# Latent heads' output projection in three rounded terms, split beside the first projection

## Chip, cores and metric

The kernel runs on one core of one Trainium2 chip. The time is the device time of one execution in microseconds (us), given as the median of three runs. A profiled execution gives the trace; its own time stands beside it below. Engines are named as in the profile: PE is TensorE (PEld its weight loads), DVE VectorE, ACT ScalarE, POOL GpSimd, SP SyncE, which issues the weight loads.

## The reference

Two transformer layers (a dense feed-forward network in the first, eight experts in the second) are followed by a third block of another kind. All values are float32, 256 tokens of 1024 features. What the change touches is the same in both layers:

```python
o_na  = neighborhood_attention(...)          # 8 heads of 64: 256 x 512
o_mla = latent_attention(q_mla, k_mla, ...)  # 8 heads of 64: 256 x 512
merged = (sigmoid(g_na  + b_gate[i, :D_MODEL]) * (o_na  @ w_na_o[i])
        + sigmoid(g_mla + b_gate[i, D_MODEL:]) * (o_mla @ w_mla_o[i]))
x = _layer_norm(DEEPNORM_ALPHA * x + merged @ w_out[i], ln1_g[i], ln1_b[i])
```

## The kernel before

Activations lie feature-major: a tile is 128 features by 256 tokens, and `o_na` and `o_mla` are four such tiles each. Each engine runs a program written out by hand, and semaphores tie them together; nothing else sets the order. Weights come through a ring of five slots of 128 x 4096 floats that SP fills in the order of `layer_plan`; a slot's next load waits until the semaphore that marks its last use has come.

Most products are made in "three rounded terms": a weight w and an input x are each split into a rounded part (type fp32r, "short") and the remainder ("rest"), and PE adds short x short, short x rest and rest x short. Making the short part is a copy (ACT, DVE or POOL), making the rest is a subtraction (DVE or POOL), written in place over the weights in the ring (`ring_lo`, `weights_rest` in the profile). A few products are still plain float32 matmuls, which the profile records as two entries each; they go through the helper `product` (L905).

After the sixteen attention heads, worked off in pairs, each layer makes sixteen output-projection tiles on PE: eight of `o_na` with `w_na_o`, then eight of `o_mla` with `w_mla_o`, each of four plain float32 matmuls (`heads_tiles`). They go into two PSUM banks in turn (`dve_bank`): a tile may start when DVE has finished with the tile two before it (`dve_tile_done`). Two tiles of `o_na` are made before the last pair's value products (L998), the others after.

DVE copies the value products out of PSUM (`output`, L2221), the last pair's as the last step of `attention`. Then it multiplies each `o_na` tile by its gate (L2528), and for each `o_mla` tile multiplies by the gate (L2542), adds the two (L2543, after which the bank is free), rounds the sum (L2535) and makes its rest (L2539), the latter two one and two tiles late.

ACT meanwhile takes the sigmoid of both gate tensors (L1847), makes `alpha_ident` for the residual (L1848) and the short parts of the first two halves of `w_out` (L1855); POOL subtracts to get their rests (L803), waiting for `act_w_short`. On PE, `residual_rows` (L1042) and `merged_rows` (L1056) follow the sixteenth tile.

Of the kernel before, what the change touches and what calls it, by code (L numbers as in the profile page):

```python
# [32 lines left out]
ACT = mybir.ActivationFunctionType  # L33
AX_X = mybir.AxisListType.X

P = 128
SEQ = 256
QT = SEQ // P
D = 1024
DT = D // P  # L40
# [55 lines left out]
RING = SLOTS - 2  # L96
IN_UNITS = 6 + 4 + 8
# [143 lines left out]
def build(nc, t):  # L241
    with ExitStack() as ctx:
# [6 lines left out]
        def parts(name, of, shape, first=0):  # L249

            return nc.alloc_sbuf_tensor_at(name, shape, F32R, offset=base_of[of] + 4 * first)

        def sem(name):
            return ctx.enter_context(nc.semaphore(name))


        ring = sb("weight_ring", [P, SLOTS, SLOT])
# [7 lines left out]
        probs = sb("probs", [P, 2, QT, SEQ])  # L265
# [18 lines left out]
        def tiles(ap, n):  # L284
            return ap.rearrange("p (t s) -> p t s", t=n)

        def const(name):
            return consts[:, slice(*CONST_AT[name])]
# [4 lines left out]
        ring_lo = [parts(f"weights_rest{i}", "weight_ring", [P, SLOT], SLOT * i) for i in range(SLOTS)]  # L293
# [16 lines left out]

        in_x = [parts(name, "weight_ring", [P, DT, SEQ], SLOT * RING + 2048 * i) for i, name in enumerate(("layer_in_short", "layer_in_rest"))]
        lat_x = [parts("latents_short", "arena_o", [P, DT, SEQ]), parts("latents_rest", "probs", [P, DT, SEQ])]
        in_w = [parts(f"layer_weights_short{b}", "weight_ring", [P, 2048], SLOT * (RING + 1) + 2048 * b) for b in range(2)]

        ff_silu = arena_mla[:, 2048:3072].rearrange("p (b s) -> p b s", b=2)
# [121 lines left out]
        first_rows_here = sem("first_rows_here")  # L437
        y_stored, y_picked, y_summed = sem("y_stored"), sem("y_picked"), sem("y_summed")
        put_picked, put_turned, put_ready = sem("put_picked"), sem("put_turned"), sem("put_ready")
        last_y, last_scattered, turn_added = [sem(f"last_y{i}") for i in range(2)], sem("last_scattered"), sem("turn_added")  # L440
        y_weighed, place_moved = sem("y_weighed"), sem("place_moved")
        moe_x_short, moe_x_ready = sem("moe_x_short"), sem("moe_x_ready")
# [113 lines left out]
        ple_block_at = [loads_of(plan) - 3]  # L556
# [81 lines left out]
        def weights_landed(block):  # L638
            return weights_here[block % RING], 32 * (block // RING + 1)
# [235 lines left out]
        def _(pe):  # L875
            n = Counts()

            def weights(k, cols, landed=True):

                i = n.block  # L880
                n.block += 1
                if landed:
                    pe.wait_ge(weights_here[i % RING], 32 * (i // RING + 1))
                return ring[:, i % RING, 0:k * cols].rearrange("p (k n) -> p k n", k=k)
# [375 lines left out]
            for l in range(LAYERS):  # L1260
# [70 lines left out]
                def heads_tiles(o, j0, j1):  # L1331
                    for j in range(j0, j1):
                        product(dve_bank()[:, 0:SEQ], cols(heads_w[-1], j * P, (j + 1) * P), k_tiles(o, 4)).then_inc(dve_tile_ready, 1)
# [14 lines left out]
                assert layer_turn_ps[l][1] is dve_ps[(n.d + 1) % 2]  # L1348
                attention(layer_pairs * l, layer_pairs, beside_pair, layer_turn_ps[l])
                heads_tiles(o_na, 2, DT)  # L1350
                heads_w.append(weights(4, D))
                pe.wait_ge(out_copied, layer_pairs * (l + 1))
                heads_tiles(o_mla, 0, DT)
                residual_rows(l)
                merged_rows(l, lambda k: (merged_split, DT * l + k + 1))
                i = n.block
# [259 lines left out]
        def _(act):  # L1616
# [181 lines left out]
            for l in range(LAYERS):  # L1798
# [46 lines left out]
                act.wait_ge(act_tile_done, n.a)  # L1845
                for g in gates:
                    nc.scalar.activation(g[:, :, :], g[:, :, :], ACT.Sigmoid).then_inc(merge_gates_ready, 1)  # L1847
                nc.scalar.activation(alpha_ident, const("ident"), ACT.Copy, scale=ALPHA).then_inc(alpha_ready, 1)  # L1848
                units = layer_units(l)

# [229 lines left out]
        def _(dve):  # L2080
# [3 lines left out]
            def ready():  # L2084
                i = n.d
                n.d += 1
                dve.wait_ge(dve_tile_ready, i + 1)
                return dve_ps[i % 2]
# [65 lines left out]
            def rms_norm(out, src, gain):  # L2154

                for j in range(DT):
                    V.scalar_tensor_tensor(out[:, j, :], src[:, j, :], gain[:, j:j + 1], std[:, 1, :], ALU.mult, ALU.mult)\
                        .then_inc(rms_ready, 1)

            def attention(first, pairs, between=None, fill=None, ahead=None, lag=1):  # L2160
                def maxima(a):
                    j = jobs[a]
# [47 lines left out]
                            m = V.tensor_scalar(p, p, rinv[:, b, i:i + 1], None, ALU.mult)  # L2210
                    m.then_inc(probs_ready, 1)

                def output(p):
                    j = jobs[2 * p]
                    dve.wait_ge(pv_ready, p + 1)
                    src = out_ps[:, p % 2 * SEQ:(p % 2 + 1) * SEQ]
                    if j["add"]:
                        dve.wait_ge(out_copied, p)
                        V.tensor_tensor(j["out"], j["out"], src, ALU.add).then_inc(out_copied, 1)
                    else:  # L2220
                        V.tensor_copy(j["out"], src).then_inc(out_copied, 1)  # L2221

                for p in range(pairs + 1):
                    at = 2 * (first + p)
                    if lag == 2 and 2 <= p < pairs:
# [11 lines left out]
                            fill(p)  # L2237
                    if lag == 1 and p:
                        output(first + p - 1)
                for p in range(pairs - 2, pairs if lag == 2 else 0):  # L2240
                    output(first + p)

            a_tiles = [0]

# [214 lines left out]
            for l in range(LAYERS):  # L2459
# [64 lines left out]
                attention(layer_pairs * l, layer_pairs, fill=lambda p: in_rest(l, 11) if p == 0 else gate_rest(l, p + 1) if p < layer_pairs - 1 else None, lag=2)  # L2524
                act_tiles(QT + 2 * DT)
                dve.wait_ge(merge_gates_ready, 2 * l + 1)
                for j in range(DT):
                    V.tensor_tensor(merged[:, j, :], ready()[:, 0:SEQ], gates[0][:, j, :], ALU.mult).then_inc(dve_tile_done, 1)  # L2528
                dve.wait_ge(merge_gates_ready, 2 * l + 2)
                merged_at = n.d  # L2530

# [351 lines left out]
```

## Time and profile before

| | us |
|---|---|
| median of 3 runs | 2029.85 |
| lowest and highest | 2029.56, 2030.17 |
| profiled execution, its own time | 2030.13 |
| its span in the trace | 2028.3 |
| PE busy | 1990.2 (98% of the span) |
| DVE busy | 1535.9 (76%) |
| ACT busy | 1012.3 (50%) |
| POOL busy | 79.9 (4%) |

The profiled execution's time is its span and 1.8 us around it. Busy shares are means over many stages. The stretch that matters here is some 35 us long and comes twice, about 170 to 207 us and 614 to 651 us from the span's start.

### The profile page before, as it was taken

To read this page: it belongs to the slowest core of one execution; us is meant where nothing else is said; L and a number is where in the kernel's file an instruction comes from. 1 tells how busy PE (TensorE), PEld (TensorE's weight loads), DVE (VectorE), ACT (ScalarE), POOL (GpSimd) and SP (SyncE) were. 2 spreads that over 40 slices of the span, in tenths; PEclk is the share of its full clock that TensorE was granted. 3 is DMA by queue.
4 is the path that set the end of the run, shared out by engine and by line. 5 is a ranking of instruction groups with operands and counts; after the bars stand their busy time and mean duration, and the time that the engine had idled before them with its cause. 6 is when DMAs were issued, how large, how long until landed. Compare 5 with 4: busy or idle time off the path is not lost.

```text
span 2028.3 us, 28426 instructions
## 1 busy us (share of the span) xinstructions
PE 1990.2 (98%) x11368; PEld 1714.6 (85%) x11368; DVE 1535.9 (76%) x1541; ACT 1012.3 (50%) x1064; POOL 79.9 (4%) x57
## 2 busy tenths in 40 slices
PE   8999999999999989999999999999999998999999
PEld 8988799989988778888888888888888877869998
DVE  3674677776654698888888888888888976567766
ACT  0363110011452377777777777777777753472000
POOL 0111100000001200000000000000001000100000
PEclk9999999999999999999999999999999999999999
DMA  9643588744634689999999999999999984435550
GB/s 328 197 152 110 184 297 307 270 148 129 218 125 151 235 297 384 381 379 371 385 385 375 385 381 380 370 384 385 377 384 380 408 284 151 145 105 178 196 176 33
DMA packets 184221, 553.22 MB, mean 273 GB/s; under 512 B 9296, under 2 KB 112080, under 8 KB 140864
## 3 DMA queue, kind: packets, MB, share of 16 engines
q1 hardware_dynamic: 175296, 517.55, 69.7%
q10 hardware_dynamic: 6912, 25.02, 3.0%
q0 software_dynamic: 1920, 9.34, 1.2%
q8 instruction: 66, 1.08, 0.2%
q14 instruction: 27, 0.22, 0.0%
HBM read 528.02 MB, written 23.59 MB: 272 GB/s over the span
## 4 chain that ended last, share of the span: by engine, by line
PE 95%; DVE 3%; ACT 2%; issue 1%; DMA 0%; DVEq 0%; ACTq 0%; SPq 0%
PE act_ps L1168 29%; PE dve_ps L1193 15%; PE act_ps L1029 15%; PE dve_ps L1029 9%; PE job_ps L1123 6%; PE dve_ps L905 6%; PE act_ps L1076 2%; PE job_ps L1056 2%; PE act_ps L905 1%; PE job_ps L1176 1%; PE job_ps L956 1%; PE job_ps L998 1%; PE job_ps L984 1%; PE act_ps L1455 1%; PE act_ps L1301 1%
## 5 line engine op out<-in xcount | busy, mean ns | idle before, releaser
L2388 DVE TENSOR_TENSOR weights_rest<-weight_ring,expert_short 128x2048 fp32r<-128x2048 f32 x336 | 763.0, 2290 | 103.1 <-ACT expert_short L1720 102.5
L1720 ACT ACTIVATE expert_short<-weight_ring 128x2048 fp32r<-128x2048 f32 x336 | 641.1, 1916 | 109.8 <-PE act_ps L1168 74.0
L1168 PE MATMUL act_ps<-expert_short,tokens_short 128*128 128x512 f32 x896 | 354.2, 395 | 4.0 <-ACT arena_o L1737 2.1
L1168 PE MATMUL act_ps<-expert_short,tokens_rest 128*128 128x512 f32 x896 | 349.2, 390 | 0.0
L1168 PE MATMUL act_ps<-weights_rest,tokens_short 128*128 128x512 f32 x896 | 349.1, 390 | 0.0
L1628 ACT ACTIVATE arena_mla<-act_ps 128x256 f32<-128x256 f32 (+1 forms) x72 | 31.0, 432 | 377.3 <-PE act_ps L1029 335.8
L1168 PEld LDWEIGHTS act_ps<-expert_short,tokens_short 128*128 128x128 f32 x896 | 168.2, 188 | 38.7 <-DVE weights_rest L2388 3.2
L1168 PEld LDWEIGHTS act_ps<-expert_short,tokens_rest 128*128 128x128 f32 x896 | 168.2, 188 | 36.2
L1168 PEld LDWEIGHTS act_ps<-weights_rest,tokens_short 128*128 128x128 f32 x896 | 168.4, 188 | 33.6
L2317 DVE TENSOR_TENSOR weights_rest<-weight_ring,ffn_weights_short 128x2048 fp32r<-128x2048 f32 x66 | 151.3, 2292 | 2.2
L1193 PE MATMUL dve_ps<-expert_short,hidden_short 128*128 128x512 f32 x448 | 139.5, 393 | 0.0
L1193 PE MATMUL dve_ps<-weights_rest,hidden_short 128*128 128x512 f32 x448 | 138.1, 390 | 0.0
L1193 PE MATMUL dve_ps<-expert_short,hidden_rest 128*128 128x512 f32 x448 | 138.1, 389 | 0.0
L1029 PE MATMUL act_ps<-layer_in_short,layer_weights_short 128*128 128x256 f32 x432 | 124.1, 287 | 1.2 <-ACT work L1628 1.2
L1029 PE MATMUL act_ps<-layer_in_rest,layer_weights_short 128*128 128x256 f32 x432 | 122.2, 283 | 0.0
L1029 PE MATMUL act_ps<-layer_in_short,weights_rest 128*128 128x256 f32 x432 | 122.1, 283 | 0.0
L2309 DVE CAST ffn_weights_short<-weight_ring 128x2048 fp32r<-128x2048 f32 x64 | 78.4, 1225 | 53.5 <-PE act_ps L1029 26.9
L1029 PE MATMUL dve_ps<-ffn_in_short,ffn_weights_short 128*128 128x256 f32 x352 | 99.7, 283 | 0.0
L1029 PE MATMUL dve_ps<-ffn_in_rest,ffn_weights_short 128*128 128x256 f32 x352 | 99.6, 283 | 0.0
L1029 PE MATMUL dve_ps<-ffn_in_short,weights_rest 128*128 128x256 f32 x352 | 99.6, 283 | 0.0
L1193 PEld LDWEIGHTS dve_ps<-weights_rest,hidden_short 128*128 128x128 f32 x448 | 84.1, 188 | 17.7
L1193 PEld LDWEIGHTS dve_ps<-expert_short,hidden_rest 128*128 128x128 f32 x448 | 84.1, 188 | 17.7
(408 smaller groups left out, 3721.1 us busy)
## 6 DMA issues: line engine op xcount, KB each, us to landing
weight_ring<-in_moe_w SPq DMA_DIRECT2D x336, 1024.0 KB, 7.0
weight_ring<-in_w_in SPq DMA_DIRECT2D x43, 1024.0 KB, 8.0
weight_ring<-in_ffn_w SPq DMA_DIRECT2D x32, 1024.0 KB, 7.6
weight_ring<-in_w_out SPq DMA_DIRECT2D x12, 1024.0 KB, 6.4
weight_ring<-in_w_gate SPq DMA_DIRECT2D x11, 1024.0 KB, 5.5
weight_ring<-in_w_up SPq DMA_DIRECT2D x11, 1024.0 KB, 8.0
weight_ring<-in_w_down SPq DMA_DIRECT2D x10, 1024.0 KB, 7.0
weight_ring<-in_w_ple_gate SPq DMA_DIRECT2D x8, 1024.0 KB, 6.5
```

What stands on the lines that cost most here:

```text
L905: m = nc.tensor.matmul(out, lhs[k], rhs[k], start=first and k == 0, stop=last and k == len(lhs) - 1)
L1029: m = nc.tensor.matmul(out, a[:, k, at], x_parts[x_part][:, first_k + k, :], start=(k == i == 0), stop=(k == steps - 1 and i == 2))
L1056: m = nc.tensor.matmul(acc_ps[2 * i + u // 2][:, :], merged_parts[a][:, 4 * c + k, i * P:(i + 1) * P], w[:, k, :], start=False, stop=(c == ...
L1076: m = nc.tensor.matmul(bank[:, :], ff_x[a][:, 4 * c + k, r * P:(r + 1) * P], w[:, k, :], start=(c == k == p == 0), stop=(c == 1 and k == 3 ...
L1123: m = nc.tensor.matmul(acc_ps[b][:, :], ff_h[h][:, pair % 4, k, r], w[:, k, half], start=(pair == k == i == 0 and not after), stop=(2 * pa ...
L1168: m = nc.tensor.matmul(bank[0:CAP, :], a[:, 4 * c + k, :], w[:, k, :], start=(c == k == i == 0), stop=(c == 1 and k == 3 and i == 2))
L1193: m = nc.tensor.matmul(dve_ps[n_half][0:CAP, :], h[:, g % 2, 2 * c + k, :], w[:, k, n_half * 512:(n_half + 1) * 512], start=(g == c == k = ...
L1628: nc.scalar.activation(out, bank[rows, 0:width], func, **kw).then_inc(act_tile_done, 1)
L1720: nc.scalar.activation(shorts[u % SHORTS][:, :], ring[:, slot, half], ACT.Copy).then_inc(moe_w_short, 1)
L2309: V.tensor_copy(ff_w[u % 2][:, :], ring[:, block % RING, half]).then_inc(ffn_w_short, 1)
L2317: V.tensor_tensor(ring_lo[block % RING][:, half], ring[:, block % RING, half], ff_w[u % 2][:, :], ALU.subtract)\
L2388: V.tensor_tensor(ring_lo[slot][:, half], ring[:, slot, half], shorts[u % SHORTS][:, :], ALU.subtract)\
```

## The change

In both layers the eight `o_mla` tiles are made of twelve rounded matmuls each instead of four plain ones. The rounded heads (`o_x`: `heads_short`, `heads_rest`, in the memory of `probs` and `probsT`) are made by DVE. The short weights go into the two buffers `in_w` (`layer_weights_short` in the profile), written by ACT; the rests are made in place in the ring by DVE, in two halves, after the third and the fifth `o_na` tile. `output` for the last pair is taken out of `attention` and comes after the second `o_na` tile.

```diff
@@ PE
                 heads_tiles(o_na, 2, DT)
-                heads_w.append(weights(4, D))
-                pe.wait_ge(out_copied, layer_pairs * (l + 1))
-                heads_tiles(o_mla, 0, DT)
+                heads_rest = tiles(ring_lo[n.block % RING][:, :], 4)
+                n.block += 1
+                pe.wait_ge(heads_split, l + 1)
+                for j in range(DT):
+                    bank, at = dve_bank(), slice(j * P, (j + 1) * P)
+                    for k in range(4):
+                        if j == 0 and k % 2 == 0:
+                            pe.wait_ge(heads_w_split, 2 * l + k // 2 + 1)
+                        short = tiles(in_w[k // 2][:, :], 2)[:, k % 2, at]
+                        for i, (w, o) in enumerate(((short, 0), (short, 1), (heads_rest[:, k, at], 0))):
+                            m = nc.tensor.matmul(bank[:, 0:SEQ], w, o_x[o][:, k, :], start=(k == i == 0), stop=(k == 3 and i == 2))
+                    m.then_inc(dve_tile_ready, 1)
@@ ACT
                     nc.scalar.activation(g[:, :, :], g[:, :, :], ACT.Sigmoid).then_inc(merge_gates_ready, 1)
+                heads_block = ple_block_at[l] - 3
+                act.wait_ge(*weights_landed(heads_block))
+                for c in range(2):
+                    act.wait_ge(*in_units(l)[IN_UNITS - 2 + c][2])
+                    nc.scalar.activation(in_w[c][:, :], ring[:, heads_block % RING, c * 2048:(c + 1) * 2048], ACT.Copy)\
+                        .then_inc(heads_w_short, 1)
@@ DVE
-                for p in range(pairs - 2, pairs if lag == 2 else 0):
-                    output(first + p)
+                if lag == 2:
+                    output(first + pairs - 2)
...
                 for j in range(DT):
                     V.tensor_tensor(merged[:, j, :], ready()[:, 0:SEQ], gates[0][:, j, :], ALU.mult).then_inc(dve_tile_done, 1)
+                    if j == 1:
+                        output(layer_pairs * (l + 1) - 1)
+                        dve.wait_ge(out_copied, layer_pairs * (l + 1))
+                        V.tensor_copy(o_x[0][:, :, :], o_mla).then_inc(heads_short, 1)
+                        dve.wait_ge(heads_short, l + 1)
+                        V.tensor_tensor(o_x[1][:, :, :], o_mla, o_x[0][:, :, :], ALU.subtract).then_inc(heads_split, 1)
+                    if j in (2, 4):
+                        heads_rest(j // 2 - 1)
```

`heads_rest(c)` waits for `heads_w_short` and subtracts half c of the short weights from the ring's, as `gate_rest` does.

How the instructions stand on DVE in layer 0, before: the copy of the last two pairs' values (x2), eight gate multiplications, then the second half's pattern.

```order
L2221 COPY arena_o<-job_ps 128x256 [waits pv_ready] x2
L2528 TENSOR_TENSOR work<-dve_ps,work 128x256 [waits dve_tile_ready,merge_gates_ready,act_tile_done]
L2528 TENSOR_TENSOR work<-dve_ps,work 128x256 [waits dve_tile_ready] x7
L2542 TENSOR_TENSOR tmp<-dve_ps,pre_norm 128x256 [waits dve_tile_ready,merge_gates_ready]
L2543 TENSOR_TENSOR work<-work,tmp 128x256 [waits dve_step]
```

The same place after the change (lines are the changed kernel's; L2553 is the former L2528, L2186 the former L2221, L2575 and L2576 the former L2542 and L2543):

```order
L2186 COPY arena_o<-job_ps 128x256 [waits pv_ready]
L2553 TENSOR_TENSOR work<-dve_ps,work 128x256 [waits dve_tile_ready,merge_gates_ready,act_tile_done]
L2553 TENSOR_TENSOR work<-dve_ps,work 128x256 [waits dve_tile_ready]
L2186 COPY arena_o<-job_ps 128x256 [waits pv_ready]
L2557 CAST heads_short<-arena_o 128x1024 [waits out_copied]
L2559 TENSOR_TENSOR heads_rest<-arena_o,heads_short 128x1024 [waits heads_short]
L2553 TENSOR_TENSOR work<-dve_ps,work 128x256 [waits dve_tile_ready]
L2550 TENSOR_TENSOR weights_rest_49<-weight_ring,layer_weights_short_64 128x2048 [waits heads_w_short]
L2553 TENSOR_TENSOR work<-dve_ps,work 128x256 [waits dve_tile_ready] x2
L2550 TENSOR_TENSOR weights_rest_49<-weight_ring,layer_weights_short_65 128x2048 [waits heads_w_short]
L2553 TENSOR_TENSOR work<-dve_ps,work 128x256 [waits dve_tile_ready] x3
L2575 TENSOR_TENSOR tmp<-dve_ps,pre_norm 128x256 [waits dve_tile_ready,merge_gates_ready]
```

Two multiplications now stand ahead of the last copy, and the split of the heads and two weight subtractions stand between the others.

On ACT in layer 0, before, from the two sigmoids on:

```order
L1847 ACTIVATE work<-work 128x2048 [waits act_tile_done]
L1847 ACTIVATE pre_norm<-pre_norm 128x2048
L1848 ACTIVATE std<-consts_sb 128x128
L1855 ACTIVATE ffn_weights_short_68<-weight_ring 128x2048 [waits weights_here1,pv_ready]
L1855 ACTIVATE ffn_weights_short_69<-weight_ring 128x2048 [waits weights_here1]
```

The same after the change (`ffn_weights_short` are the copies that POOL's subtractions wait for, L1873 the former L1855):

```order
L1859 ACTIVATE work<-work 128x2048 [waits act_tile_done]
L1859 ACTIVATE pre_norm<-pre_norm 128x2048
L1864 ACTIVATE layer_weights_short_64<-weight_ring 128x2048 [waits act_tile_ready,weights_here0]
L1864 ACTIVATE layer_weights_short_65<-weight_ring 128x2048 [waits act_tile_ready]
L1866 ACTIVATE std<-consts_sb 128x128
L1873 ACTIVATE ffn_weights_short_70<-weight_ring 128x2048 [waits weights_here1,pv_ready]
L1873 ACTIVATE ffn_weights_short_71<-weight_ring 128x2048 [waits weights_here1]
```

The two heads' weight copies stand ahead of the copies that POOL waits for. POOL's own order is unchanged.

## Rows read from the trace of the kernel before

**Rows 1.** The page's part 4: the chain that ended last, by engine.
```profile
PE 95%; DVE 3%; ACT 2%; issue 1%; DMA 0%; DVEq 0%; ACTq 0%; SPq 0%
```

**Rows 2.** The chain in order of time, 165 to 235 us: start, us, what.
```profile
165.63 5.75 PE act_ps L1029 x48
...
178.74 24.44 PE dve_ps L905 x112
203.19 3.57 PE job_ps L1042 x32
...
233.71 1.64 DVE ffn_in_short L2148
```

**Rows 3.** Timeline of DVE: start us, us, instruction, count, idle time before and its releaser.
```profile
177.94 0.42 DVE L2221 COPY arena_o<-job_ps 128x256 f32<-128x256 f32 x1 [5.07 <-PE job_ps L998]
178.28 0.74 DVE L2528 TENSOR_TENSOR work<-dve_ps,work 128x256 f32<-128x256 f32 x2
180.78 0.42 DVE L2528 TENSOR_TENSOR work<-dve_ps,work 128x256 f32<-128x256 f32 x1 [1.75 <-PE dve_ps L905]
...
191.21 0.42 DVE L2542 TENSOR_TENSOR tmp<-dve_ps,pre_norm 128x256 f32<-128x256 f32 x1 [1.37 <-PE dve_ps L905]
191.66 0.43 DVE L2543 TENSOR_TENSOR work<-work,tmp 128x256 f32<-128x256 f32 x1
...
203.22 0.42 DVE L2542 TENSOR_TENSOR tmp<-dve_ps,pre_norm 128x256 f32<-128x256 f32 x1 [0.30 <-PE dve_ps L905]
```

**Rows 4.** Timeline of ACT at the same place.
```profile
175.41 1.91 ACT L1847 ACTIVATE work<-work 128x2048 f32<-128x2048 f32 x1
...
179.03 0.29 ACT L1848 ACTIVATE std<-consts_sb 128x128 f32<-128x128 f32 x1
...
179.23 1.89 ACT L1855 ACTIVATE ffn_weights_short<-weight_ring 128x2048 fp32r<-128x2048 f32 x1
...
181.03 1.89 ACT L1855 ACTIVATE ffn_weights_short<-weight_ring 128x2048 fp32r<-128x2048 f32 x1
```

**Rows 5.** Timeline of POOL, three places in layer 0.
```profile
139.64 3.10 POOL L780 TENSOR_TENSOR arena_bias<-arena_bias,consts_sb 128x384 f32<-128x384 f32 x3
...
181.20 9.01 POOL L803 TENSOR_TENSOR weights_rest<-weight_ring,ffn_weights_short 128x2048 fp32r<-128x2048 f32 x2 [38.46 <-ACT ffn_weights_short L1855]
...
230.67 4.53 POOL L803 TENSOR_TENSOR weights_rest<-weight_ring,ffn_weights_short 128x2048 fp32r<-128x2048 f32 x1
```

**Rows 6.** DVE beside POOL: timeline; one line's instructions (ns min/median/max).
```profile
141.81 3.09 DVE L2285 TENSOR_TENSOR weights_rest<-weight_ring,layer_weights_short 128x2048 fp32r<-128x2048 f32 x1
...
L2148 DVE CAST ffn_in_short<-residual x8: 279/280/1644, 233.7 to 238.5; 128x256 fp32r<-128x256 f32 x8
```

**Rows 7.** Two DVE lines of 2048 columns: ns min/median/max, first and last start.
```profile
L2258 DVE CAST layer_weights_short<-weight_ring x6: 1217/1218/1228, 29.5 to 59.5; 128x2048 fp32r<-128x2048 f32 x6
...
L2484 DVE TENSOR_TENSOR layer_in_rest<-residual,layer_in_short x1: 2281/2281/2281, 22.6 to 22.6; 128x2048 fp32r<-128x2048 f32 x1
```

**Rows 8.** Timeline of PE: the first rounded matmul behind plain ones, and its successor.
```profile
35.72 0.47 PE L1029 MATMUL act_ps<-layer_in_short,layer_weights_short 128*128 128x256 f32 x1
36.03 0.28 PE L1029 MATMUL act_ps<-layer_in_rest,layer_weights_short 128*128 128x256 f32 x1
```

**Rows 9.** PE's timeline; windows (us, PE, PEld, DVE, ACT, POOL busy, granted clock, DMA).
```profile
453.17 0.63 PE L935 MATMUL act_ps<-consts_sb,pre_norm 128*128 128x128 f32 x4 [2.38 <-DVE pre_norm L2114]
...
1678.74 0.66 PE L935 MATMUL dve_ps<-consts_sb,pre_norm 128*128 128x128 f32 x4 [3.81 <-DVE pre_norm L2114]
...
453.95:457.25 3.30, 3.30 (x15) 3.03 (x14) 2.03 (x8) 2.35 (x6) 0.00 (x0) 0.50 1.10 348
1679.40:1682.60 3.20, 3.20 (x14) 2.84 (x14) 2.51 (x7) 1.20 (x3) 0.00 (x0) 0.50 0.88 350
```

**Rows 10.** Layer 1: timeline of DVE, and of POOL.
```profile
621.93 0.42 DVE L2221 COPY arena_o<-job_ps 128x256 f32<-128x256 f32 x1 [5.07 <-PE job_ps L998]
...
625.26 9.00 POOL L803 TENSOR_TENSOR weights_rest<-weight_ring,ffn_weights_short 128x2048 fp32r<-128x2048 f32 x2 [384.74 <-ACT ffn_weights_short L1855]
```

More of the change, by code:

```diff
@@ L312, in build @@
         lat_x = [parts("latents_short", "arena_o", [P, DT, SEQ]), parts("latents_rest", "probs", [P, DT, SEQ])]
+        o_x = [parts("heads_short", "probs", [P, 4, SEQ]), parts("heads_rest", "probs", [P, 4, SEQ], 4 * SEQ)]
         in_w = [parts(f"layer_weights_short{b}", "weight_ring", [P, 2048], SLOT * (RING + 1) + 2048 * b) for b in range(2)]
@@ L439, in build @@
         put_picked, put_turned, put_ready = sem("put_picked"), sem("put_turned"), sem("put_ready")
+        heads_short, heads_split = sem("heads_short"), sem("heads_split")
+        heads_w_short, heads_w_split = sem("heads_w_short"), sem("heads_w_split")
         last_y, last_scattered, turn_added = [sem(f"last_y{i}") for i in range(2)], sem("last_scattered"), sem("turn_added")
@@ L2158, in rms_norm, with output @@
                         .then_inc(rms_ready, 1)
+            def output(p):
+                j = jobs[2 * p]
+                dve.wait_ge(pv_ready, p + 1)
+                src = out_ps[:, p % 2 * SEQ:(p % 2 + 1) * SEQ]
+                if j["add"]:
+                    dve.wait_ge(out_copied, p)
+                    V.tensor_tensor(j["out"], j["out"], src, ALU.add).then_inc(out_copied, 1)
+                else:
+                    V.tensor_copy(j["out"], src).then_inc(out_copied, 1)
             def attention(first, pairs, between=None, fill=None, ahead=None, lag=1):
@@ L2211, in normalise @@
                     m.then_inc(probs_ready, 1)
[L2213 to L2221, printed above, removed]
                 for p in range(pairs + 1):
@@ L2526, in _, with heads_rest @@
                 dve.wait_ge(merge_gates_ready, 2 * l + 1)
+                def heads_rest(c):
+                    block = ple_block_at[l] - 3
+                    half = slice(c * 2048, (c + 1) * 2048)
+                    dve.wait_ge(heads_w_short, 2 * l + c + 1)
+                    V.tensor_tensor(ring_lo[block % RING][:, half], ring[:, block % RING, half], in_w[c][:, :], ALU.subtract)\
+                        .then_inc(heads_w_split, 1)
                 for j in range(DT):
                     V.tensor_tensor(merged[:, j, :], ready()[:, 0:SEQ], gates[0][:, j, :], ALU.mult).then_inc(dve_tile_done, 1)
+                    if j == 1:
[6 more added lines that the diff above has]
+                        heads_rest(j // 2 - 1)
                 dve.wait_ge(merge_gates_ready, 2 * l + 2)
```

## The prediction

> **What bounds the kernel now.** The page comes first: TensorE (PE) is busy for 98% of the span and holds 95% of the chain of work that ended last [rows 1]. So I read the one stretch that the change touches, once in each of two layers. The chain of waits [rows 2] gives its shape in layer 0: PE is released by VectorE (DVE) at 178.74, works off fourteen output-projection tiles (24.44 us, 112 records, two for each plain f32 matmul), adds the residual from 203.19, and goes on to the next projection (L1056). From the first of them to the residual that is 24.2 us for fourteen, 1.73 us a tile once the pipe is filled. Whatever moves the residual's start moves everything behind it, since PE is on the chain there and the later loads, splits and norms all hang on PE. Layer 1 repeats the pattern 443.99 us later (its last copy is at 621.93, layer 0's at 177.94 [rows 3, 10]; POOL's two subtractions take 9.0 us there too), so I work out one layer and double it.
>
> DVE's timeline [rows 3] shows slack in the first half: a gate multiplication (L2528) takes 0.42 us and then waits. In the second half it does four instructions per tile (L2542, L2543, L2535, L2539) and waits 0.30 us before each tile (203.22) at PE's pace of 1.73, so it needs 1.43. From the start of a tile on PE (178.74) to DVE's read of it (180.78) are 2.04 us.
>
> **The front: two tiles ahead of the copy.** Now PE's third tile waits for DVE's first multiplication, and that stands behind the last copy, 177.94 to 178.7. In the changed order the multiplication waits only for the gates, ready at 175.41 + 1.91 = 177.32 [rows 4]. It is done by 177.8, when PE comes out of its value products; PE's third tile starts at 177.82 instead of 178.74: -0.92 us. DVE's second tile is at 177.70, the copy at 178.04, so nothing waits for it longer than for the splits.
>
> **The splits, and the first new wait.** After the copy DVE rounds the heads (1024 columns) and subtracts. No row has these sizes: the cast lies between 0.28 us (256 columns) and 1.22 (2048), the subtraction between 0.43 and 2.28 [rows 3, 6, 7]; on the line between the ends they are 0.69 and 1.22. DVE reaches tile 2 (counted from 0) at 180.4. ACT now makes two rounded weight halves straight after its second sigmoid, that is at 179.03, where `alpha_ident` stands now; a copy of this size takes 1.89 us and its successor starts 1.80 later [rows 4]: ready at 180.92 and 182.7. DVE's first weight subtraction (2.28, the next starts some 2.2 later) runs from 180.95, tiles 3 and 4 follow at 183.16 and 183.50, the second subtraction at 183.84 to 186.1, tile 5 at 186.05. PE's tiles start at 177.82, 179.55, 181.28; tile 5 could start at 183.0, but needs the bank of tile 3, free at 183.6: +0.6 us. Tiles 6 and 7 start at 185.35 and 187.08, and the new product at 188.81, with all of its inputs there since 186.1.
>
> **The new product.** Twelve rounded matmuls per tile replace four plain ones. 48 such matmuls take 5.75 us [rows 2], so a tile is 1.44 instead of 1.73: 8 x 0.29 = -2.3 us. The first rounded matmul after plain ones starts its successor 0.31 us later instead of 0.12 [rows 8]: +0.2. DVE's 1.43 per tile still fits under 1.44. So far a layer gains 0.92 - 0.6 + 2.3 - 0.2 = 2.4 us.
>
> **What is pushed back: GpSimd.** ACT's two weight copies stand ahead of its copies for L1056, and these move from 179.23 to 182.83. GpSimd (POOL) subtracts behind each of them: today from 181.20, two in 9.0 us, 4.5 us each, ended at 190.2 [rows 5], before DVE's second half begins at 191.21 [rows 3]. In the changed kernel POOL is released at about 184.8. What then happens is read elsewhere in the trace. POOL's three bias additions end at 142.74, and a DVE subtraction of two SBUF tiles beside them took 3.09 us instead of 2.28: it ended as if begun when POOL had ended. A DVE cast of 0.28 us took 1.64 beside POOL's L803, from 233.71 to 235.35, and POOL ended at 235.20 [rows 2, 5, 6]. DVE's multiplications that take one input from PSUM kept 0.42 beside POOL's 9.0 us (180.78) [rows 3]. So DVE and POOL take turns, a whole instruction at a time, when DVE reads two SBUF tiles or casts from SBUF to SBUF. The Trainium skill, page "SBUF — State Buffer", section "SBUF: two separate sides", says the same: the port pair shared by the two is an exclusive lock that the first to start keeps for its whole instruction, for DVE instructions in a 2-port mode or with two SBUF inputs. By that rule the trace agrees; without it the sum would stay at the gain above.
>
> POOL, released at 184.8, finds DVE in its second weight subtraction until 186.1, so its two instructions run to about 190.5 and 195.0. PE's tile 8 starts at 188.81, is read by DVE (L2542, one PSUM input, not held) at 190.63, and the addition behind it (L2543, two SBUF tiles) wants to start at 191.09: 0.5 us too late to slip in between the two POOL instructions. It is held until 195.0 and ends at 195.3. PE has only two banks: it finishes tile 9 at 191.88 and waits for that addition until 195.34, **3.5 us**. From then on it is the bound again. Per layer: -2.4 + 3.5 = **+1.05 us**; the residual starts at about 204.2 instead of 203.19.
>
> **The clock.** A PE wait of 2.38 us that ended at 453.17 and one of 3.81 us that ended at 1678.74 were each followed, within 0.8 us, by at least 3.2 us at a granted clock of 0.50, the 1.2 GHz level of the two [rows 9]. A wait of 3.5 us lies between them. Such a stretch costs half its length if PE works all through it, 1.7 us, and less if it begins while PE still waits; nothing if it doesn't come. I take 1.3 us per layer, ends 0 and 1.7.
>
> **Sum.** 2 x (1.05 + 1.3) = +4.7 us on the profiled execution's 2030.13. The median stands 0.28 lower, so the forecast is 2029.85 + 4.7 = **2034.5 us**. No other queue pays: SP's loads are released by tiles that come within 1 us of today's times, the alpha copy on ACT is needed only at 204, and POOL's results at 190.5 and 195.0 are needed after 207.
>
> **Rivals.**
> (a) DVE isn't held: L2543 goes through beside POOL, or POOL is the one that waits. For: POOL's second subtraction has 10 us to spare. Against: both blocked rows above. PE tile 10 starts at 191.88, the residual at 200.8; the layer gains 2.4, no low clock: 2029.85 - 4.8 = 2025.0. Chance 0.12.
> (b) DVE slips in between POOL's two instructions, because it is 0.5 us earlier or POOL later than worked out. The addition of tile 8 is on time, but that of tile 9 is held until 195.3 and ends at 195.6. PE waits 2.4 us, five tiles remain (7.2), and the residual starts about when it does now: 2029.8, or up to 2032.4 with the low clock in both layers. Chance 0.13.
> (c) POOL gets in before DVE's second weight subtraction. The margin is 184.8 - 183.84 = 1 us; it decides if DVE is later than that. Then the subtraction waits for 189.3, tile 5 of DVE moves to 191.5, PE stands still from 187.1 to 191.9, and the residual starts 2.3 us late, with a low clock behind it: 4 us a layer, 2038. Chance 0.07.
> (d) The forecast's case: chance 0.68, its own range 2031.5 (no low clock) to 2036.0 (both layers, full price).
>
> **How the numbers follow.** The range takes in (d) and (b) and leaves (a) and (c), 0.19: 2029.6 to 2036.3. About 0.2% (4.06 us) is what a measurement of this kernel can tell from no change. Slower by more than that is (c) and those cases of (d) whose clock losses add up to 2 us or more, about 0.6 of it: 0.07 + 0.41 = 0.48. Faster is (a): 0.12. The rest, 0.40, is (b) and (d) with little lost clock. The mechanism itself points to a loss; whether it is one that can be measured hangs on the clock.
>
> **What would show it.** In the changed profile, in both layers: the third tile's wait for DVE gone; rounded matmuls at 1.44 us a tile; a PE wait of about 3.5 us inside the new product, its releaser a DVE addition onto `work`; that addition's record some 4.2 us long instead of 0.43, ending 0.2 to 0.3 us after POOL's second subtraction; POOL's first subtraction about 5.7 us long, since it waits for DVE; a granted clock of 0.5 behind the wait. A record of 0.43 us throughout would be (a); one long record on the second tile's addition only, (b); a long weight subtraction on DVE, (c). The forecast is wrong above all if DVE isn't held, or if POOL ends well before 195.

## The result, and the profile after

| | before, us | after, us |
|---|---|---|
| median of 9 runs each | 2029.71 | 2036.0 |
| lowest and highest | 2028.25, 2030.61 | 2034.07, 2037.3 |
| profiled execution | 2030.13 | 2034.07 |
| its span | 2028.3 | 2032.2 |
| DVE busy | 1535.9 | 1554.9 |

The changed kernel is 1.003 times as long as the one before (95% interval 1.0021 to 1.0038), which is 4.3 to 7.7 us longer with 6.3 in the middle. The forecast was 2034.5 us, 4.7 us longer, with a range of 2029.6 to 2036.3. Sign and mechanism are right; the middle is 1.5 us too low.

Every step of the forecast can be looked up in layer 0. In this run the last value products start at 177.12 us instead of 176.80, so 0.3 us is to be taken off each time below before it is set beside one of before. DVE's timeline (start us, us, instruction, count, and in brackets idle time before and what ended it), against [rows 3]:

```profile
177.73 0.76 DVE L2553 TENSOR_TENSOR work<-dve_ps,work 128x256 f32<-128x256 f32 x2 [4.54 <-ACT work L1859]
...
181.28 2.29 DVE L2550 TENSOR_TENSOR weights_rest<-weight_ring,layer_weights_short 128x2048 fp32r<-128x2048 f32 x1
...
184.15 2.28 DVE L2550 TENSOR_TENSOR weights_rest<-weight_ring,layer_weights_short 128x2048 fp32r<-128x2048 f32 x1
...
190.94 0.42 DVE L2575 TENSOR_TENSOR tmp<-dve_ps,pre_norm 128x256 f32<-128x256 f32 x1 [1.07 <-PE dve_ps L1364]
191.40 4.22 DVE L2576 TENSOR_TENSOR work<-work,tmp 128x256 f32<-128x256 f32 x1
```

The addition (L2576, L2543 before) takes 4.22 us where it took 0.43 [rows 3]. A record ten times too long is a wait: here the trace puts the time in which the engine is held into the instruction itself, and names no releaser. What holds it is found on POOL's timeline, on the same time axis:

```profile
185.12 10.21 POOL L806 TENSOR_TENSOR weights_rest<-weight_ring,ffn_weights_short 128x2048 fp32r<-128x2048 f32 x2 [41.90 <-ACT ffn_weights_short L1873]
```

POOL's two subtractions start at 185.12 instead of 181.20 [rows 5]. They take 10.2 us instead of 9.0, since the first must wait for DVE's second weight subtraction to end (184.15 + 2.28), and end at 195.33; DVE's addition ends at 195.62. PE's timeline, and its waits over the whole run (idle us in total, times, the longest):

```profile
183.96 5.45 PE L908 MATMUL dve_ps<-arena_o,weight_ring 128*128 128x256 f32 x24 [0.30 <-DVE work L2553]
```

```profile
PE dve_ps L1364 <- DVE work L2576: 6.8, 2, 3.4
```

And the chain of waits in order of time, for both layers, against [rows 2]:

```profile
183.96 5.45 PE dve_ps L908 x24
189.41 1.44 PE dve_ps L1364 x12
...
191.40 4.24 DVE work L2576
195.63 0.04 issue
195.68 10.16 PE dve_ps L1364 x72
205.83 3.57 PE job_ps L1045 x32
...
636.50 4.24 DVE work L2576
...
640.77 10.39 PE dve_ps L1364 x72
651.16 3.57 PE job_ps L1045 x32
```

The first tile of the new product takes 1.44 us for its twelve matmuls. The six tiles behind the wait (72 matmuls) take 10.16 and 10.39 us; at full clock this piece takes 8.89, as the third experiment shows. Windows (their ends and length in us, busy time and count of PE, granted clock, DMA share, GB/s) say why:

```profile
195.00:196.00 1.00, 0.32 (x1) 0.56 1.05 397
196.00:198.00 2.00, 2.00 (x11) 0.50 0.26 95
198.00:199.00 1.00, 1.00 (x8) 0.73 0.00 0
642.00:643.00 1.00, 1.00 (x8) 0.63 0.00 0
643.00:645.00 2.00, 2.00 (x11) 0.50 0.01 4
```

Around the end of each wait of 3.41 us the granted clock fell to 0.50, PE's 1.2 GHz level, and that costs 10.16 - 8.89 = 1.3 us in layer 0, where the clock fell while PE was still waiting (the window from 195.00 has 0.32 us of work), and 10.39 - 8.89 = 1.5 in layer 1, where PE was at work again.

One measure serves for all kernels: the time from the start of the last pair's value products to the start of the residual's matmuls. In the kernel before it runs from

```profile
176.80 1.08 PE L998 MATMUL job_ps<-probsT,arena_gate 128*64 128x256 f32 x8
...
203.02 3.73 PE L1042 MATMUL job_ps<-std,residual 128*128 128x128 f32 x32
```

that is 26.22 us in layer 0 (26.21 in layer 1), and in the changed one from 177.12 to 205.67, 28.55, and from 622.22 to 651.0, 28.8. The stretch is longer by 2.3 and 2.6 us. The forecast said 2.35 for each.

### The profile page after: what moved, and what is told of

The parts are those of the page before. It is cut to its first block, busy times and chain, and to the rows that moved or that the text cites. A ratio compares the mean times of both kernels' runs of the same rounds, so it can differ in the third digit from the quotient of the medians.

```text
span 2032.2 us, 28568 instructions
## 1 busy us (share of the span) xinstructions
PE 1988.3 (98%) x11432; PEld 1714.4 (84%) x11432; DVE 1554.9 (77%) x1549; ACT 1019.4 (50%) x1068; POOL 82.5 (4%) x57
## 4 chain that ended last, share of the span: by engine, by line
PE 93%; DVE 3%; ACT 2%; issue 1%; DMA 0%; DVEq 0%; ACTq 0%; SPq 0%
PE act_ps L1171 29%; PE dve_ps L1196 15%; PE act_ps L1032 15%; PE dve_ps L1032 9%; PE job_ps L1126 6%; PE dve_ps L908 3%; PE act_ps L1079 2%; PE job_ps L1059 2%; PE act_ps L908 1%; PE job_ps L1179 1%; PE dve_ps L1364 1%; PE job_ps L959 1%; PE job_ps L1001 1%; PE job_ps L987 1%; PE act_ps L1467 1%
```

## The experiments

Theory: POOL, released 3.9 us later, collides with DVE's additions; DVE is held for a whole instruction of POOL, PE waits for DVE and gets a low clock on top. Rivals: the gain of the product isn't there at all; the wait comes from the added work on DVE and not from POOL; the clock costs nothing. The runs of before that the experiments were compared with have a median of 2029.85 (first four) and 2030.04 us (last four).

**POOL's second subtraction out of the way.** It waits until DVE has made the last rest, so that only one instruction of POOL lies in the stretch. (In the diffs `...` marks lines left out, and "@@" says where a piece stands.)

```diff
@@ POOL, in front of its subtraction
+                        if i == 1:
+                            pool.wait_ge(merged_split, DT * (l + 1))
```

> The changed kernel, with one wait more on POOL: the second of its two subtractions for the output projection (L806) waits until DVE has made the last rest of the merged tiles. Theory L (DVE and POOL take turns when DVE reads two SBUF tiles): DVE's addition onto work is never long (0.43 us instead of 4.22), PE doesn't wait inside the new product, no stretch of low clock follows, and the residual starts near 200.8 on layer 0's time axis instead of 205.8. POOL's second subtraction then runs from about 203.3 to 207.8 and is needed at about 210. Against the kernel before: 2 x -2.4 us, about 2025. Rival D (DVE has simply more work than fits, 6.9 us a layer, and PE waits for it whatever POOL does): the wait of 3.4 us stays and the time stays near 2036.

Measured: 2025.87 us, ratio 0.9981 (0.9972 to 0.999). POOL's timeline, then the chain:

```profile
185.53 5.73 POOL L808 TENSOR_TENSOR weights_rest<-weight_ring,ffn_weights_short 128x2048 fp32r<-128x2048 f32 x1 [38.03 <-ACT ffn_weights_short L1875]
203.80 4.60 POOL L808 TENSOR_TENSOR weights_rest<-weight_ring,ffn_weights_short 128x2048 fp32r<-128x2048 f32 x1 [12.54 <-DVE merged_rest L2574]
```

```profile
184.37 5.45 PE dve_ps L910 x24
189.82 11.51 PE dve_ps L1366 x96
201.33 3.57 PE job_ps L1047 x32
```

The 96 rounded matmuls now run through in 11.51 us, as forecast for eight tiles of 1.44, with no wait and no low clock. DVE does exactly the work that it does in the changed kernel. So some 10 us (2036.0 against 2025.87) hang on the place of one POOL instruction, and the wait doesn't come from DVE's added work. The stretch is 23.63 us in both layers, 2.6 shorter than before; the time is 0.9 us above the 2025 that was expected.

**The bank given back early.** The multiplication, not the addition behind it, now returns the PSUM bank; the addition counts on a semaphore of its own, for which the rounding of the sum waits, and is held as before.

```diff
...
-                    step(V.tensor_tensor(tmp[:, j % 2, :], ready()[:, 0:SEQ], gates[1][:, j, :], ALU.mult))
-                    V.tensor_tensor(merged[:, j, :], merged[:, j, :], tmp[:, j % 2, :], ALU.add).then_inc(dve_tile_done, 1)
+                    V.tensor_tensor(tmp[:, j % 2, :], ready()[:, 0:SEQ], gates[1][:, j, :], ALU.mult).then_inc(dve_tile_done, 1)
+                    dve.wait_ge(dve_tile_done, n.d)
+                    V.tensor_tensor(merged[:, j, :], merged[:, j, :], tmp[:, j % 2, :], ALU.add).then_inc(merged_added, 1)
```

> The changed kernel, but DVE gives PE's bank back after the multiplication that reads it, and not after the addition behind it. Theory L: the addition is still held for 4.2 us, but PE has one tile more to work on meanwhile, so its wait shrinks from 3.4 us to about 2.3 (the held addition now delays the reading of the next tile instead). Per layer 1.1 to 1.4 us less than the changed kernel, and up to 1.7 more if the low clock stays away: 2030 to 2033.8. Rival D: DVE's work isn't less, so only the order of its waits changes, and the time stays within 1 us of 2036.

Measured: 2030.6 us, ratio 1.001 (1.0001 to 1.0019). DVE's timeline, then the chain in layer 0 and, from 639.38, in layer 1:

```profile
190.72 4.26 DVE L2577 TENSOR_TENSOR work<-work,tmp 128x256 f32<-128x256 f32 x1
```

```profile
195.37 7.45 PE dve_ps L1364 x60
202.82 3.24 PE job_ps L1045 x29
...
639.38 8.95 PE dve_ps L1364 x60
```

The hold is the same length, 4.26 us, but PE gets one tile further before it must wait, and waits 2.34 us instead of 3.41. The stretch in layer 0 is 26.22 us, what it was before the change; in layer 1 it is 27.71. Sixty matmuls take 7.45 us in one layer and 8.95 in the other: a wait of the same length was followed by a low clock in one and not in the other, worth 1.5 us.

**PE kept busy through the wait.** 26 rounded matmuls into an unused bank, whose results nobody reads, stand in front of the third tile of the new product.

```diff
+                    if j == 2:
+                        pe.wait_ge(act_tile_done, n.a)
+                        for _ in range(26):
+                            nc.tensor.matmul(act_ps[0][:, 0:SEQ], in_w[0][:, 0:P], o_x[0][:, 0, :], start=True, stop=True)
```

> The changed kernel with 26 matmuls more on PE in each layer, of 128x256 rounded operands into an unused bank, their results thrown away, put where PE waits inside the new product. At 0.12 us each they take 3.1 of the 3.4 us of that wait. If the stretch of low clock behind the wait comes from PE standing idle, it is gone, and each layer gains the 1.5 and 1.8 us that it cost: 2036.0 - 3.3 = 2032.7. If it comes from something else, the stretch stays and the time is 2036 or a little more.

Measured: 2032.82 us, ratio 1.0016 (1.0007 to 1.0025). DVE's timeline, the chain and a window of PE behind it:

```profile
191.86 4.29 DVE L2580 TENSOR_TENSOR work<-work,tmp 128x256 f32<-128x256 f32 x1
```

```profile
196.21 8.89 PE dve_ps L1368 x72
205.10 1.01 PE job_ps L1045 x9
```

```profile
196.00:198.00 2.00, 1.79 (x15) 1.00 0.49 184
```

The hold is untouched, all but 0.4 us of PE's idle time is gone, the granted clock stays at 1.00, and the 72 matmuls take 8.89 us. The stretch is 27.36 us in layer 0 and 27.38 in layer 1: without the clock the change costs 1.14 us in layer 0 (the forecast said 1.05). The median is 3.2 us below that of the changed kernel, where the traces put 1.3 and 1.5 on the clock (the expectation had put 1.5 and 1.8 there). This run's profile had longer low stretches elsewhere, in code that the edit doesn't touch, so that its profiled time (2036.03) lies above its median.

**POOL's copies first.** ACT makes `alpha_ident` and the two copies for POOL ahead of the two heads' weight copies, so that POOL has its old place.

```diff
-                heads_block = ple_block_at[l] - 3
...
-                        .then_inc(heads_w_short, 1)
@@ behind the copies for POOL
+                heads_block = ple_block_at[l] - 3
...
+                        .then_inc(heads_w_short, 1)
```

> The changed kernel with ACT's order turned round: first alpha_ident and the two copies that POOL waits for, then the two copies for the heads' weights. POOL is released at about 181.5 as in the kernel before. Theory L: POOL has the port first. DVE's first weight subtraction, ready at about 184.9, is held until 185.9, the second until POOL's second subtraction ends near 192.6; PE waits for banks and for the second half of the weights, and the residual starts near 206 or later, with a low clock behind the waits: 2037 to 2040, no better than the changed kernel although POOL is done before the merged tiles begin. Rival D, or a lock that bites only on additions onto work: POOL is out of the way before those, the only cost is a start of the weight subtractions some 4 us later, and the time falls below 2033.

Measured: 2042.41 us, ratio 1.0065 (1.005 to 1.0081), the slowest of all. The timelines of DVE and of PE, and two windows of PE:

```profile
184.52 3.13 DVE L2550 TENSOR_TENSOR weights_rest<-weight_ring,layer_weights_short 128x2048 fp32r<-128x2048 f32 x1 [3.94 <-ACT layer_weights_short L1876]
187.57 0.74 DVE L2553 TENSOR_TENSOR work<-dve_ps,work 128x256 f32<-128x256 f32 x2
188.23 5.92 DVE L2550 TENSOR_TENSOR weights_rest<-weight_ring,layer_weights_short 128x2048 fp32r<-128x2048 f32 x1
```

```profile
188.03 8.50 PE L908 MATMUL dve_ps<-arena_o,weight_ring 128*128 128x256 f32 x24 [4.94 <-DVE work L2553]
```

```profile
187.00:190.00 3.00, 1.97 (x5) 0.52 0.00 0
190.00:193.00 3.00, 3.00 (x9) 0.50 0.00 0
```

The time is 2.4 us above the upper end of what was expected. The heads' weight subtractions come late and into POOL's way: the records are 3.13 and 5.92 us long for instructions of 2.28. But the two don't weigh the same. PE's wait of 4.94 us ends with the multiplications at 187.57, behind the first of them. DVE had stood idle for 3.94 us in front of it, until ACT's late copy came, and was then held for 0.85. So most of this wait is the copies' new place, and not a hold. The long hold of 5.92 us, the one that the rival (c) describes, begins when PE is at work again, and PE's timeline shows no further wait in layer 0: its clock of 0.50, from 187 to beyond 193, stretches the tiles over it, 8.50 us for the 24 records that take 5.45 in the changed kernel. The run shows that weight subtractions are held like additions; it doesn't give the price of (c). The two stretches are 31.32 and 31.39 us.

In the changed kernel (c) stays away because DVE's second weight subtraction starts at 184.15 and POOL at 185.12, the 1 us that the prediction named.

**The output's new place alone.** The kernel before, with the last copy behind the second multiplication and nothing else.

```diff
...
-                for p in range(pairs - 2, pairs if lag == 2 else 0):
-                    output(first + p)
+                if lag == 2:
+                    output(first + pairs - 2)
@@ the gate multiplications
+                    if j == 1:
+                        output(layer_pairs * (l + 1) - 1)
```

> The kernel before, with one part of the change alone: VectorE reads two tiles ahead of the last copy. The plain product stays and nothing is split. PE's third tile starts when its value products end instead of 0.92 us later, and no split lies in the way afterwards: 2 x -0.9 = -1.8 us, about 2028.0. Rival: the wait only moves to a later tile; then the time stays at 2029.8.

Measured: 2027.94 us, ratio 0.9991 (0.9982 to 1.0). The stretch goes from 177.39 to 202.76, 25.37 us, and is 25.37 in layer 1: 0.85 less than before in each. The median is 2.1 us lower (by its interval 0 to 3.7), the trace gives 1.7.

**ACT's two copies alone.** The kernel before, with plain matmuls and no split, but with the two heads' weight copies on ACT, which PE waits for and doesn't use. It delays POOL as the change does.

```diff
@@ PE, in front of the o_mla tiles
+                pe.wait_ge(heads_w_short, 2 * (l + 1))
@@ ACT, behind the sigmoids
...
+                for c in range(2):
+                    act.wait_ge(*in_units(l)[IN_UNITS - 2 + c][2])
+                    nc.scalar.activation(in_w[c][:, :], ring[:, heads_block % RING, c * 2048:(c + 1) * 2048], ACT.Copy)\
+                        .then_inc(heads_w_short, 1)
```

> The kernel before, with only ACT's two copies of the heads' weights added in their place; PE waits for them long after they are there, and nobody uses them. They do nothing but put POOL's release off by 3.8 us, to about 185. Theory L: POOL runs from 185 to 194, so DVE's addition for the ninth tile, due at 191.7, is held until 194.0 and PE waits some 1.6 us for its bank, in each layer: +3.2 us, about 2033, and more if a low clock follows. Rival D (it is DVE's own added work): DVE does no more here than in the kernel before, so 2029.8.

Measured: 2034.71 us, ratio 1.0027 (1.0017 to 1.0037). Timelines of POOL, DVE and PE:

```profile
185.09 9.01 POOL L804 TENSOR_TENSOR weights_rest<-weight_ring,ffn_weights_short 128x2048 fp32r<-128x2048 f32 x2 [39.09 <-ACT ffn_weights_short L1863]
```

```profile
191.95 2.43 DVE L2551 TENSOR_TENSOR work<-work,tmp 128x256 f32<-128x256 f32 x1
```

```profile
194.44 10.63 PE L906 MATMUL dve_ps<-arena_o,weight_ring 128*128 128x256 f32 x48 [1.32 <-DVE work L2551]
```

With no subtraction of DVE in its way POOL takes 9.01 us and ends at 194.10; the addition ends at 194.38. Two copies on an engine that is busy half the time, with no consumer, cost 1.6 us a layer in the trace (27.81 and 27.88 us against 26.22 and 26.21) and 4.7 in the median. The trace explains 3.3 of these, just under the interval's lower end of 3.5. The granted clock behind the waits of 1.32 and, in layer 1, 1.39 us stayed at 1.00 here.

**The first experiment without the output's new place.** POOL's second subtraction waits as there, and the last copy is back in `attention`.

```diff
-                if lag == 2:
-                    output(first + pairs - 2)
+                for p in range(pairs - 2, pairs if lag == 2 else 0):
+                    output(first + p)
@@ the gate multiplications
-                        output(layer_pairs * (l + 1) - 1)
```

> The kernel of e1 (POOL's second subtraction waits), but with the last copy back in attention, ahead of all gate multiplications. If the two tiles ahead are worth here what they are worth alone, this is 1.8 us slower than e1, about 2027.7. My working says less: with the splits in place, PE's sixth tile waits for DVE, whose chain starts with ACT's sigmoids and weight copies and doesn't depend on when PE's third tile starts. So only 0.3 to 0.4 us a layer are lost: about 2026.5.

Measured: 2027.11 us, ratio 0.9986 (0.9977 to 0.9995). PE's timeline, and below it the same place in the first experiment:

```profile
179.29 10.63 PE L910 MATMUL dve_ps<-arena_o,weight_ring 128*128 128x256 f32 x48 [0.86 <-DVE work L2555]
189.57 0.47 PE L1366 MATMUL dve_ps<-heads_short,layer_weights_short 128*128 128x256 f32 x1
```

```profile
178.62 5.45 PE L910 MATMUL dve_ps<-arena_o,weight_ring 128*128 128x256 f32 x24
189.47 0.47 PE L1366 MATMUL dve_ps<-heads_short,layer_weights_short 128*128 128x256 f32 x1
```

PE waits 0.86 us for its third tile, and then runs six tiles in one piece: the wait of 0.30 at the sixth, which the changed kernel has, is gone. From the third tile to the first rounded matmul it is 10.28 us here and 10.85 with that wait, so it costs 0.57 us, more than the 0.30 in which PE is idle. Stretches of 23.92 and 23.91 us against 23.63: the new place is worth 0.85 us a layer alone, and 0.3 beside the splits by the trace (1.2 for both layers by the medians; the two expectations were 0.3 to 0.4 and 0.9 a layer). DVE's splits cost the rest: of the 0.85 that PE gains at the third tile, it gives 0.57 back at the sixth.

**Both mends.** The first experiment with the bank given back early as well.

> The kernel of e1 with the early return of the banks from e2. In e1 PE doesn't wait for a bank inside the new product, so Theory L expects no further gain: within 1 us of e1's 2025.9. If early return had helped e2 for another reason than the held addition, it would help here too, by 1 to 2 us.

Measured: 2025.22 us, ratio 0.9975 (0.9964 to 0.9985); the stretch of layer 1 goes from 618.53 to 642.16, 23.63 us, as in the first experiment. Where no addition is held, the early return is worth nothing that can be seen. The profiled execution took 2029.26 us, more than all seven others (2024.1 to 2026.1); where that lies is shown below the next table. This kernel and the first experiment's are the fastest here, faster than the one before and the changed one.

**The runs together.** In us; "two stretches" is the sum over both layers against the kernel before:

| kernel | two stretches | median against before |
|---|---|---|
| changed | +4.9 | +6.3 |
| POOL's second waits | -5.2 | -4.0 |
| bank early | 0.0 in layer 0, +1.5 of clock in layer 1 | +0.8 |
| wait filled | +2.3 | +3.0 |
| POOL's copies first | +10.3 | +12.6 |
| output alone | -1.7 | -2.1 |
| ACT's copies alone | +3.3 | +4.7 |
| POOL's second waits, no new place | -4.6 | -2.9 |
| both mends | -5.2 | -4.8 |

The order is the same in both columns; a median stands between 0.7 below and 2.3 above its two stretches. What varies outside them is the clock. The longest piece that neither the change nor an experiment touches goes from the residual of layer 1 to the last value products of the program. It takes 1168.2 us in the profile before and 1168.1 in that of the changed kernel, but between 1166.8 (POOL's second waits) and 1172.2 (both mends) in the ten profiles. Windows of PE in these two, the first kernel's above:

```profile
680.70:684.00 3.30, 3.30 (x17) 0.50 0.85 360
642.63:1809.43 1166.80, 1146.65 (x5562) 1.00 0.89 339
```

```profile
679.80:689.90 10.10, 9.21 (x32) 0.50 0.32 136
1772.00:1775.30 3.30, 3.04 (x16) 0.50 0.80 252
642.16:1814.32 1172.16, 1152.41 (x5562) 0.99 0.88 337
```

Both kernels have stretches of 23.6 us, and their profiled executions took 2024.39 and 2029.26 us: the 5.4 us between them in this piece are more than that whole difference. Single executions of one kernel fall into groups in the same way: of the kernel before, those at a mean granted clock of 0.998 took 2028.3 to 2028.9 us, those at 0.996 and 0.997 2029.3 to 2031.1, two at 0.995 2033.4 and 2033.7; of the changed kernel those at 0.996 took 2034.1 and 2034.3, the four at 0.993 2036.6 to 2037.3. How often low clock comes elsewhere in the program differs from run to run by more than what is left to explain here.

## Why the prediction was right, step by step

- **The front.** Forecast 0.92 us a layer, measured 0.85 (alone). DVE's two multiplications started at 177.73 - 0.3 = 177.4 (177.32 forecast), and PE went straight on.
- **The wait at the sixth tile.** Forecast 0.6, measured 0.57 (10.85 us from the third tile to the first rounded matmul against 10.28 without the wait); the 0.30 in PE's row is only the time in which PE is idle. Both weight subtractions took 2.28 us as read from the table of sizes; the tile started at 183.96, the forecast's 183.6 in the shifted time.
- **The product.** Forecast -2.3 and +0.2. Where nothing is held, the first rounded matmul starts at 189.47 and the residual at 201.16, 11.69 us, against 13.8 for eight tiles of 1.73: 2.1 to 2.2 us. Right. Together a layer gains 2.6 there (forecast 2.4).
- **POOL's release and the lock.** Forecast 184.8, 190.5 and 195.0; measured 185.12, 185.12 + 5.73 = 190.85 (5.73 is the first subtraction's time in the first experiment) and 195.33, exact when the 0.3 is taken off. DVE's addition wanted to start at 191.40, 0.55 us too late to come between POOL's two (forecast 0.5), which is what kept the rival (b) away. Its record was forecast at "some 4.2 us", measured 4.22; it ends 0.29 us behind POOL's. The held additions have records of 4.22, 4.26, 4.29 and 2.43 us, each ending 0.3 us behind POOL's, and the multiplication with one PSUM input kept 0.42 beside POOL in all of these runs. In the Trainium skill, page "SBUF — State Buffer", section "SBUF: two separate sides", the port pair that DVE and GpSimd share is a lock for whole instructions. The records agree with it.
- **PE's wait.** Forecast 3.5, measured 3.41 of idle time in both layers. Without the clock layer 0 costs 1.14 (wait-filled kernel), forecast 1.05. That is closer than its parts: the gain was 0.2 us larger than forecast, and so was what the hold takes away (27.36 - 23.63 = 3.7 us), and the two cancel.
- **The clock.** Forecast 1.3 us a layer, ends 0 and 1.7; measured 1.3 and 1.5 in the profiled execution. So both stretches together are 4.9 us longer, against 4.7 forecast. That a low clock came in both layers was in part luck: the forecast rested on two rows of one profile. The wait of 2.38 us was followed by it in only six of the ten profiles, and the wait of 3.81 us in nine; in the kernel with POOL's copies first the clock stayed at 1.00 from its end, 1687.5, to 1694.
- **The profiled execution.** It stands only 3.9 us above the one before, though the two stretches alone cost 4.9. Elsewhere a low stretch is missing: in front of the next section PE waits 2.38 us [rows 9] and 2.37 us here, for the same instruction, and this time no low clock followed:

```profile
455.84 0.63 PE L938 MATMUL act_ps<-consts_sb,pre_norm 128*128 128x128 f32 x4 [2.37 <-DVE pre_norm L2132]
```

```profile
453.00:457.00 4.00, 1.63 (x14) 1.00 1.11 349
```

From the residual of layer 0 to the value products of layer 1, a piece that the change doesn't touch, it is 620.80 - 203.02 = 417.78 us before, and 622.22 - 205.67 = 416.55 here: 1.2 us less for one low stretch that didn't come. That is the difference between 4.9 and the profile's 3.9, but for some tenths at the start (177.12 against 176.80). The ten profiles fall into the same two groups: 417.8 us in the six with the low clock, 416.5 to 416.6 in the four without.
- **The median.** This is where the forecast is off. It took the sum on one profiled execution as the shift of the median. The median moved by 6.3, 1.4 us more than the two stretches. The forecast had no term for the clock of the rest of the program, which put the ten profiles up to 5.4 us apart in one piece that nothing touches. That the 1.4 us lie there fits the mean clock of the nine executions (0.993 to 0.996, where before had mostly 0.996 to 0.998), of which the two waits themselves account for 0.0017; but the two profiles have this piece equally long, no run isolates the rest, and it stays open.

Of the rivals, the price of (a) was right: without a hold the kernel takes 2025.87 (2025.0 worked out). So was the price that (b) put on a PE wait of 2.4 us, 2029.8 to 2032.4: the early bank return has waits of 2.34 and takes 2030.6. The price of (c), 2038, wasn't tested. The kernel with POOL's copies first has a PE wait of 4.94 us where (c) had 4.8, but for another reason, the late copies on ACT, and its 2042.4 is no measure of (c).

## What to carry to other kernels

When work is added to an engine that is off the chain, follow what it delays to the end: here two copies on ACT, busy half the time, moved a POOL instruction by 3.9 us into the path of DVE's additions, and that cost more than the faster product gained. Look for DVE instructions with two SBUF inputs, or casts from SBUF to SBUF (0.28 us took 1.64 in [rows 6]), beside a POOL instruction, and place POOL's with a wait where DVE has none of them; the cure was one wait. Give PSUM banks back with the instruction that reads them, not with the one behind it, and count a wait of PE at its length plus half of the low clock that may come with it.

## What the runs showed of the hardware

A PE wait doesn't settle whether a low clock follows. After the waits of 3.41 us it came both times (1.3 and 1.5 us lost), after two of 2.34 us once (7.45 against 8.95 us for 60 matmuls). At one and the same place of the program, a wait of 2.37 to 2.38 us was followed by it in six profiles of ten [rows 9], and one of 3.81 us in nine. After 1.32 and 1.39 us it didn't come. Nor does a low clock need a wait in front of it: in the kernel before it was 0.50 from 686.1 to 692.8 (the first window here), after 39 us in which PE was busy for 38.9 (the second), toward their end in part with matmuls of only 8 columns.

```profile
686.10:692.80 6.70, 5.60 (x17) 0.50 0.27 114
646.90:686.00 39.10, 38.85 (x202) 1.00 0.78 302
```

Matmuls whose results are thrown away kept the clock at 1.00 through a hold of 4.29 us and gave back 3.2 us in the median, though they do nothing else.
